# Where the second gather's rows lie within blocks of 32 partitions

## The chip, the cores and the metric

The kernel runs on one core of a Trainium2 chip. The metric is the time of one execution on the device, in microseconds (us). Before the change three runs took 2975.83 to 2976.99 us, with a median of 2976.5 us.

## What is computed

Two layers on 256 tokens of width 2048, everything in float32. The first is a convolution block with a feed-forward block; the second is attention, a pooling branch and, at its end, a layer of small experts. Only this last layer is touched by the change. For each token and each of 8 heads it chooses 16 of 16384 experts, takes a row of 2048 numbers for each from a table U, and, with the weights so found, adds up the same rows of a second table V:

```python
u = jnp.take(expert_u, idx, axis=0)
a = jnp.einsum('thkd,td->thk', u, xb)
hid = jax.nn.gelu(a) * g
vsel = jnp.take(expert_v, idx, axis=0)
return jnp.einsum('thk,thkd->td', hid, vsel)
```

That is 256 x 8 x 16 = 32768 (token, head, slot) choices, each with a row of U and the same row of V, 8 KB each.

## The kernel before, in words

**Which rows are gathered.** The kernel handles the 16384 experts in two ways. Those of the last 40 of 128 key groups (index 88 x 128 = 11264 and up) are computed densely: their rows of U and V are streamed as whole panels of 1 MB by SyncE's queue (line 526) and multiplied by TensorE (lines 2363 and 2373). All other choices are gathered row by row. A gather is one indirect transfer of up to 128 rows into a tile of 128 partitions; an index at or over 11264 is out of its bounds, and its row isn't fetched.

**Gathers of U.** GpSimd issues 256 gathers of U (line 638). Number k belongs to group g = k // 4 and fetches one slot of one head for 128 tokens, token p into partition p. VectorE multiplies the tile with the tokens' inputs and sums (`dot`, line 1824), one tile at a time.

**Gathers of V.** GpSimd issues as many gathers of V (line 658), four for a group, each for 32 tokens and the group's four slots: slot s of the four lies in partitions 32 s to 32 s + 31. TensorE multiplies such a tile by a matrix of 128 rows and 32 columns that holds the weights (`spread`), so that each row is added to its token's output (`adds`, line 2418). The two kinds of gathers alternate: U number k, then V number k - 4. In what follows "pair k" is U number k with V number k.

**Batches.** The 16 slots of a head are four batches of four, j = 0 to 3. `four_of(g)` says which head and which batch group g is: the groups go over the heads first, so that groups of one batch follow each other. A group's heads belong to one block of 128 tokens: groups 0 to 31 to the first, 32 to 63 to the second.

**The shift.** Within a block of 32 partitions the V rows don't lie in the order of the tokens: partition p holds the row of token (p + 16) mod 32 of its block. Three places make this so. Line 1795 shuffles the expert indices of a head on VectorE after they are found (`pairs_experts`), line 1873 shuffles the weights of a group in the same way, and lines 1102 and 1109 on ScalarE build the `spread` matrix from a shifted unit matrix. Groups 17 to 31 take another way to the same matrix: line 1157 makes a diagonal of the unshuffled weights, and TensorE turns it over.

**The order of the work.** The routing of a head (its best keys, the pairs, the experts) runs on VectorE. Three heads are routed before the gathers begin; the other 13 are interleaved, one a group with some groups left out (`route_in`), in groups 1 to 6 and on to group 15, the last of their four steps being `pairs_experts`, which ends with line 1795. All engines work in the order in which they are written. A gather of U waits for its index (`expert_ready`) and for a free tile: there are 5 tiles for U, 7 from k = 136 on, and 7 tiles for V, then 8. The dense U panels come in groups 0 to 17, the dense V panels from group 34 on.

Of the kernel before, what the change touches and what calls it, by code (L numbers as in the profile page):

```python
# [33 lines left out]
PH, TOPK, NKEYS = 8, 16, 128  # L34
# [112 lines left out]
    return PH + g % PH, g // PH  # L147


SHIFTED = [(p + 16) % 32 for p in range(32)]  # L150


def route_in(g):
# [90 lines left out]
def two_layers(nc, stream, dense_u, columns, x, meta, b_out, g_mix_post, g_ffn, g_ffn_post, g_norm1, g_norm2, w_forget,  # L244
# [5 lines left out]
    K, Q = 1024, 32  # L250
# [3 lines left out]
    def place(name, shape, offset, dt=f32):  # L254
        assert name not in names
        names.add(name)
        return nc.alloc_sbuf_tensor_at(name, shape, dt, offset=offset)
# [10 lines left out]
    ident = keep("s_ident", [128, 128])  # L268
# [108 lines left out]
    def spot(n):  # L377
        size = (4 * n + 63) // 64 * 64
        for piece in room:
            if piece[0] + size <= piece[1]:  # L380
                piece[0] += size
                return piece[0] - size
        raise MemoryError(n)

    def small(name, n, dt=f32):
        return place(name, [128, n], spot(n), dt)
# [8 lines left out]
    cand = place("s_cand", [128, TOPK * TOPK], pick_at)  # L395
    cand_rest = place("s_cand_rest", [128, TOPK * TOPK], pick_at + 4 * TOPK * TOPK)
    diagonal = [place(f"s_diagonal{i}", [128, 4, Q], pick_at + 512 + 512 * i) for i in range(2)]
    iota_i = small("s_iota_i", NKEYS, mybir.dt.int32)
    iota_f = small("s_iota_f", NKEYS)
    sc_rest = small("s_sc_rest", NKEYS)  # L400
    val = small("s_val", 2 * TOPK)
# [5 lines left out]
    gsum = small("s_gsum", 4)  # L407
    expert_f = [small(f"s_expert_f{i}", TOPK) for i in range(2)]
    expert_v_f = [small(f"s_expert_v_f{i}", TOPK) for i in range(2)]
    shifted = small("s_shifted", Q)  # L410
    u_index = [small(f"s_u_index{i}", TOPK, u32) for i in range(ROUTES)]
    v_index = [small(f"s_v_index{i}", 4 * GROUPS, u32) for i in range(ROUTES)]
    gate_kept = [small(f"s_gate_kept{i}", TOPK) for i in range(ROUTES)]
# [6 lines left out]
    with ExitStack() as ctx:  # L420
# [253 lines left out]
        def _(act):  # L674
# [422 lines left out]

            for q in range(4):
                own = slice(q * Q, (q + 1) * Q)
                for half in range(2):  # L1100
                    from_half = slice(q * Q + (1 - half) * Q // 2, q * Q + (2 - half) * Q // 2)
                    ins = act.activation(shifted[own, half * Q // 2:(half + 1) * Q // 2], ident[own, from_half], ACT.Copy)
            ins.then_inc(shifted_ready, 1)
            act.wait_ge(shifted_ready, 1)

            def one_spread(g, q, s):

                own = slice(q * Q, (q + 1) * Q)
                return act.activation(spread[g % NW][s * Q:(s + 1) * Q, q, :], shifted[own, :], ACT.Copy,  # L1109
                                      scale=hid[g % NH][own, s:s + 1])  # L1110

            def spreads(g):
# [40 lines left out]
            def diagonal_of(g):  # L1153

                act.wait_ge(hid_ready, g + 1)
                for s in range(4):
                    ins = act.activation(diagonal[g % 2][:, s, :], shifted[:, :], ACT.Copy, scale=hid[g % NH][:, s:s + 1])
                ins.then_inc(diagonal_ready, 1)

            def blocks_copied(g):  # L1160
# [60 lines left out]
        def _(dve):  # L1221
# [558 lines left out]
            def pairs_experts(th):  # L1780

                step(dve.tensor_scalar(pos_of[:, 0:TOPK], pos[:, :], 4, None, ALU.logical_shift_right))
                link(dve.tensor_scalar(pos_of[:, TOPK:], pos[:, :], TOPK - 1, None, ALU.bitwise_and))
                both = pick[:, :].rearrange("p (s a) -> p s a", a=TOPK)
                halves = pick[:, :].rearrange("p (h k a) -> p h k a", h=2, a=TOPK)
                link(dve.tensor_tensor(both, iota_f[:, 0:TOPK].unsqueeze(1).to_broadcast([128, 2 * TOPK, TOPK]),
                                       pos_of[:, :].unsqueeze(2).to_broadcast([128, 2 * TOPK, TOPK]), ALU.is_equal))
                link(dve.tensor_tensor(halves, halves, ind[:, :].rearrange("p (h a) -> p h a", h=2).unsqueeze(2).to_broadcast([128, 2, TOPK, TOPK]),
                                       ALU.mult))
                keys_of = picked[th // PH][:, 0:2 * SLOTS].rearrange("p (h s) -> p h s", h=2)[:, :, th % PH * TOPK:(th % PH + 1) * TOPK]  # L1790
                link(dve.tensor_reduce(keys_of, halves, AX.X, ALU.add))
                wait(dve, v_index_ready, th - 1)
                link(dve.scalar_tensor_tensor(expert_f[th % 2][:, :], keys_of[:, 0, :], float(NKEYS), keys_of[:, 1, :], ALU.mult, ALU.add))
                link(dve.tensor_copy(u_index[th][:, :], expert_f[th % 2][:, :]))
                dve.stream_shuffle(expert_v_f[th % 2][:, :], expert_f[th % 2][:, :], SHIFTED).then_inc(expert_ready, 1)

            def gates_softmax(th):
                mine = picked[th // PH][:, 2 * SLOTS + th % PH * TOPK:][:, 0:TOPK]
# [64 lines left out]
            def hidden(g, first=0, end=BATCH):  # L1863

                th, j = four_of(g)
                dve.wait_ge(gelu_ready, g + 2 if first else g + 1)
                mine = hid[g % NH][:, first:end]
                if g in TURNED:
                    dve.tensor_tensor(mine, gelu[g % NH][:, first:end], gate_kept[th][:, j * BATCH + first:j * BATCH + end], ALU.mult)\
                        .then_inc(hid_ready, 1)  # L1870
                else:
                    link(dve.tensor_tensor(mine, gelu[g % NH][:, first:end], gate_kept[th][:, j * BATCH + first:j * BATCH + end], ALU.mult))
                    dve.stream_shuffle(mine, mine, SHIFTED).then_inc(hid_ready, 1)  # L1873


            dve.wait_ge(iota_ready, 1)
# [650 lines left out]
```

## Time and profile before

| what | us |
|---|---|
| median of 3 runs | 2976.5 |
| lowest and highest run | 2975.83, 2976.99 |
| the profiled execution's own time | 2973.8 |
| its span, first to last instruction | 2971.7 |
| first gather issued (of U) | 1804.1 |
| last gather issued (of V) | 2947.6 |
| last row packet of a gather ends, about | 2964 |

The profile is of one execution. Times inside it are counted from its first instruction. PE is TensorE, DVE VectorE, ACT ScalarE, POOL GpSimd, SP SyncE. The transfer engines (DMA) are 16; a "share" of them is the time that their packets took, divided by 16 times the stretch, and can come out slightly above 1. A row of a table is one packet of 8 KB; a row that is out of bounds, and each engine's notice that it is done, is a packet of a few bytes.

### The profile page before, as it was taken

Reading aid. Unit: us, or ns where it says so; the run is one execution under the profiler, and the core shown is the slowest. Engines: PE = TensorE matmul, PEld = TensorE weight load, DVE = VectorE, ACT = ScalarE, POOL = GpSimd, SP = SyncE. Lnnn points to the kernel's source line nnn. Section 1 sums busy time; section 2 is a strip of 40 time slices with the busy share of each in tenths; the row PEclk is TensorE's granted clock in tenths of the full one; section 3 lists DMA queues with packets and bytes.
Section 4 is the critical chain, followed back from the end, with each engine's and each line's share of the span. In section 5 each row is a group of like instructions: output and inputs, shape, how many; then the busy total and the mean of one; then the engine's idle time right before and its main releaser. Section 6 shows DMA issues by size and latency. Waiting matters only on the chain.

```text
span 2971.7 us, 45765 instructions
## 1 busy us (share of the span) xinstructions
PE 2759.5 (93%) x17115; PEld 2063.2 (69%) x17115; DVE 1917.5 (65%) x3302; ACT 1177.4 (40%) x2302; POOL 660.7 (22%) x568
## 2 busy tenths in 40 slices
PE   8999999999999997999999999999998787888885
PEld 7886778888888887989999889677764432222221
DVE  6888566655665556455444557988858885555556
ACT  1003443333333434434333445565556542223333
POOL 0000000000000000040000002454446665555554
PEclk9999999999999998999999999999996679989897
DMA  6432545555555553443455656999999999999998
GB/s 246 142 142 101 209 158 187 193 186 183 189 192 183 186 193 121 165 147 141 173 185 184 249 201 226 365 409 416 413 378 419 401 409 423 423 422 420 419 420 356
DMA packets 131299, 785.53 MB, mean 264 GB/s; under 512 B 34630, under 2 KB 34630, under 8 KB 35846
## 3 DMA queue, kind: packets, MB, share of 16 engines
q1 hardware_dynamic: 55040, 393.16, 36.0%
q0 software_dynamic: 75712, 389.74, 32.4%
q8 instruction: 94, 1.54, 0.2%
q14 instruction: 69, 0.57, 0.1%
q10 hardware_dynamic: 384, 0.52, 0.0%
HBM read 940.23 MB, written 4.19 MB: 318 GB/s over the span
## 4 chain that ended last, share of the span: by engine, by line
PE 62%; DMA 16%; DVE 12%; issue 6%; ACT 2%; POOL 2%; DVEq 1%; POOLq 0%; ACTq 0%
PE bank L1970 10%; PE bank L1964 10%; PE bank L1965 10%; PE bank L1966 10%; DMA s_u<-in_expert_u,s_u_index 10%; DMA s_v<-in_expert_v,s_v_index 6%; PE bank L2363 6%; PE bank L1971 5%; PE bank L2060 4%; DVE s_u L1824 3%; PE bank L2418 3%; PE bank L2373 2%; DVE s_cacc L1333 2%; POOL s_u L638 1%; DVE s_w_lo L1244 1%
## 5 line engine op out<-in xcount | busy, mean ns | idle before, releaser
L1244 DVE TENSOR_TENSOR s_w_lo<-s_raw,s_w_hi 128x2048 fp32r<-128x2048 f32 x258 | 592.6, 2297 | 577.0 <-ACT s_w_hi L685 576.5
L685 ACT ACTIVATE s_w_hi<-s_raw 128x2048 fp32r<-128x2048 f32 x256 | 490.4, 1916 | 750.6 <-PE bank L1966 475.2
L1970 PE MATMUL bank<-s_a,s_w_hi 128*128 128x512 f32 x1408 | 494.3, 394 | 3.2 <-DVE s_w_lo L1244 3.2
L1824 DVE CUSTOM_DVE_ANT_0 s_u<-s_u,s_xn_late 128x1024 f32<-128x1024 f32 x256 | 303.6, 1223 | 221.2 <-DMA s_u<-in_expert_u,s_u_index 195.3
L2418 PE MATMUL bank<-s_v,s_spread 128*32 128x512 f32 x2048 | 312.5, 727 | 142.2 <-DMA s_v<-in_expert_v,s_v_index 106.0
L1971 PE MATMUL bank<-s_a,s_w_lo 128*128 128x256 f32 x1408 | 395.1, 281 | 0.0
L638 POOL DMA_INDIRECT s_u<-in_expert_u,s_u_index x256 | 298.9, 1168 | 381.4 <-DVE s_halfdot L1824 222.4
L658 POOL DMA_INDIRECT s_v<-in_expert_v,s_v_index x256 | 311.5, 1217 | 206.6 <-PE bank L2418 120.3
L1824 DVE CUSTOM_DVE_ANT_0 s_u<-s_u,s_xn 128x1024 f32<-128x1024 f32 x256 | 303.0, 1223 | 46.6 <-DMA s_u<-in_expert_u,s_u_index 40.9
L1964 PE MATMUL bank<-s_a,s_w_hi 128*128 128x256 f32 x1152 | 325.1, 282 | 3.4 <-DVE s_a L1268 1.8
L1965 PE MATMUL bank<-s_a,s_w_hi 128*128 128x256 f32 x1152 | 324.4, 282 | 0.0
L1966 PE MATMUL bank<-s_a,s_w_lo 128*128 128x256 f32 x1152 | 324.0, 281 | 0.0
L1109 ACT ACTIVATE s_spread<-s_shifted,s_hid 32x32 f32<-32x32 f32 x784 | 249.4, 318 | 188.0 <-DVE s_hid L1873 169.0
L1970 PEld LDWEIGHTS bank<-s_a,s_w_hi 128*128 128x128 f32 x1408 | 264.7, 188 | 66.2 <-DVE s_w_lo L1244 6.4
L2418 PEld LDWEIGHTS bank<-s_v,s_spread 128*32 128x32 f32 x2048 | 64.0, 123 | 341.0 <-issue 284.6
L2373 PE MATMUL bank<-s_raw,s_ha 128*32 128x512 f32 x2560 | 297.1, 617 | 0.0
L2363 PE MATMUL bank<-s_xnt,s_raw 128*128 128x256 f32 x1184 | 265.2, 382 | 1.3 <-issue 0.9
L1971 PEld LDWEIGHTS bank<-s_a,s_w_lo 128*128 128x128 f32 x1408 | 264.9, 188 | 0.4
L2363 PEld LDWEIGHTS bank<-s_xnt,s_raw 128*128 128x128 f32 x1184 | 221.9, 190 | 59.6 <-issue 30.9
L2060 PE MATMUL bank<-s_a_f,s_raw 128*128 128x272 f32 x1024 | 235.2, 393 | 2.0 <-DVE s_a_f L1301 1.2
L2373 PEld LDWEIGHTS bank<-s_raw,s_ha 128*32 128x32 f32 x2560 | 94.8, 115 | 202.8 <-issue 202.0
L2060 PEld LDWEIGHTS bank<-s_a_f,s_raw 128*128 128x128 f32 x1024 | 194.4, 190 | 42.6 <-issue 2.6
(332 smaller groups left out, 3912.3 us busy)
## 6 DMA issues: line engine op xcount, KB each, us to landing
s_raw<-in_stream SPq DMA_DIRECT2D x292, 1024.0 KB, 4.8
s_raw<-in_expert_v SPq DMA_DIRECT2D x40, 1024.0 KB
s_raw<-in_dense_u SPq DMA_DIRECT2D x37, 1024.0 KB
s_u<-in_expert_u,s_u_index POOLq DMA_INDIRECT x256
s_v<-in_expert_v,s_v_index POOLq DMA_INDIRECT x256
s_panel_early<-in_dense_u POOLq DMA_DIRECT2D x3, 1024.0 KB, 11.4
s_xres<-in_x SPq DMA_DIRECT2D x2, 1024.0 KB, 5.9
out<-s_out_row SPq DMA_DIRECT2D x24, 64.0 KB
```

The costliest lines, as they stand in the source:

```text
L685: act.activation(w_hi[s % 2][:, :], raw[s][:, :], ACT.Copy).then_inc(hi_ready, 1)
L1244: dve.tensor_tensor(w_lo[s % 2][:, :], raw[s][:, :], w_hi[s % 2][:, :].bitcast(f32), ALU.subtract)\
L1824: ins = dve.tensor_tensor_reduce(out=u_slot[r][:, half], in0=u_slot[r][:, half], in1=xn_late[:, half] if t else xn[:, 0, half], scale=SHRI ...
L1964: pe.matmul(dst, left[0], right[0], start=start, stop=False)
L1965: pe.matmul(dst, left[0], right[1], start=False, stop=False)
L1966: return pe.matmul(dst, left[1], right[0], start=False, stop=stop)
L1970: pe.matmul(dst, left[0], both, start=start, stop=False)
L1971: return pe.matmul(dst[:, 0:T], left[1], both[:, 0], start=False, stop=stop)
L2060: ins = pe.matmul(bank[c][:, 0:L], raw[c % 4][:, k * 128:(k + 1) * 128], a_f[:, k, :], start=k == 0, stop=k == KT - 1)
L2363: ins = pe.matmul(bank[b][:, 0:T], source[:, k * 128:(k + 1) * 128], xnt[:, k, 0:T], start=k == 0, stop=k == KT - 1)
L2373: ins = pe.matmul(bank[4 * t + q][c * Q:(c + 1) * Q, :], ha[:, d, t * 128 + q * Q:t * 128 + (q + 1) * Q], raw[r][:, c * 512:(c + 1) * 512] ...
L2418: ins = pe.matmul(bank[4 * t + q][c * Q:(c + 1) * Q, :], spread[g % NW][:, q, :], v_slot[r][:, c * 512:(c + 1) * 512], start=False, stop=last)
```

## The change

The shift becomes a number for each batch: 16, 8, 24 and 16 for j = 0 to 3. The one shuffle of a head's 16 indices becomes four shuffles of four indices (L1795). The weights of a group are shuffled by its batch's shift (L1873). The shifted unit matrix gives way to two unit matrices side by side, `same_q`, 64 columns wide, out of which a window of 32 columns is read at the batch's shift; it lies where `iota_i` lay, which is no longer used by then. Batches 0 and 3 keep the shift that they had.

```diff
--- before.py
+++ after.py
@@ -147,7 +147,12 @@
     return PH + g % PH, g // PH
 
 
-SHIFTED = [(p + 16) % 32 for p in range(32)]
+SHIFTS = (16, 8, 24, 16)
+
+
+def shifted_by(shift):
+
+    return [(p + shift) % 32 for p in range(32)]
 
 
 def route_in(g):
@@ -395,7 +400,9 @@
     cand = place("s_cand", [128, TOPK * TOPK], pick_at)
     cand_rest = place("s_cand_rest", [128, TOPK * TOPK], pick_at + 4 * TOPK * TOPK)
     diagonal = [place(f"s_diagonal{i}", [128, 4, Q], pick_at + 512 + 512 * i) for i in range(2)]
-    iota_i = small("s_iota_i", NKEYS, mybir.dt.int32)
+    iota_at = spot(NKEYS)
+    iota_i = place("s_iota_i", [128, NKEYS], iota_at, mybir.dt.int32)
+    same_q = place("s_same_q", [128, 2 * Q], iota_at)
     iota_f = small("s_iota_f", NKEYS)
     sc_rest = small("s_sc_rest", NKEYS)
     val = small("s_val", 2 * TOPK)
@@ -407,7 +414,6 @@
     gsum = small("s_gsum", 4)
     expert_f = [small(f"s_expert_f{i}", TOPK) for i in range(2)]
     expert_v_f = [small(f"s_expert_v_f{i}", TOPK) for i in range(2)]
-    shifted = small("s_shifted", Q)
     u_index = [small(f"s_u_index{i}", TOPK, u32) for i in range(ROUTES)]
     v_index = [small(f"s_v_index{i}", 4 * GROUPS, u32) for i in range(ROUTES)]
     gate_kept = [small(f"s_gate_kept{i}", TOPK) for i in range(ROUTES)]
@@ -1097,16 +1103,15 @@
 
             for q in range(4):
                 own = slice(q * Q, (q + 1) * Q)
-                for half in range(2):
-                    from_half = slice(q * Q + (1 - half) * Q // 2, q * Q + (2 - half) * Q // 2)
-                    ins = act.activation(shifted[own, half * Q // 2:(half + 1) * Q // 2], ident[own, from_half], ACT.Copy)
+                for twice in range(2):
+                    ins = act.activation(same_q[own, twice * Q:(twice + 1) * Q], ident[own, own], ACT.Copy)
             ins.then_inc(shifted_ready, 1)
             act.wait_ge(shifted_ready, 1)
 
             def one_spread(g, q, s):
 
                 own = slice(q * Q, (q + 1) * Q)
-                return act.activation(spread[g % NW][s * Q:(s + 1) * Q, q, :], shifted[own, :], ACT.Copy,
+                return act.activation(spread[g % NW][s * Q:(s + 1) * Q, q, :], same_q[own, Q - SHIFTS[four_of(g)[1]]:2 * Q - SHIFTS[four_of(g)[1]]], ACT.Copy,
                                       scale=hid[g % NH][own, s:s + 1])
 
             def spreads(g):
@@ -1154,7 +1159,7 @@
 
                 act.wait_ge(hid_ready, g + 1)
                 for s in range(4):
-                    ins = act.activation(diagonal[g % 2][:, s, :], shifted[:, :], ACT.Copy, scale=hid[g % NH][:, s:s + 1])
+                    ins = act.activation(diagonal[g % 2][:, s, :], same_q[:, SHIFTS[four_of(g)[1]]:Q + SHIFTS[four_of(g)[1]]], ACT.Copy, scale=hid[g % NH][:, s:s + 1])
                 ins.then_inc(diagonal_ready, 1)
 
             def blocks_copied(g):
@@ -1792,7 +1797,10 @@
                 wait(dve, v_index_ready, th - 1)
                 link(dve.scalar_tensor_tensor(expert_f[th % 2][:, :], keys_of[:, 0, :], float(NKEYS), keys_of[:, 1, :], ALU.mult, ALU.add))
                 link(dve.tensor_copy(u_index[th][:, :], expert_f[th % 2][:, :]))
-                dve.stream_shuffle(expert_v_f[th % 2][:, :], expert_f[th % 2][:, :], SHIFTED).then_inc(expert_ready, 1)
+                for j in range(GROUPS):
+                    four = slice(j * BATCH, (j + 1) * BATCH)
+                    ins = dve.stream_shuffle(expert_v_f[th % 2][:, four], expert_f[th % 2][:, four], shifted_by(SHIFTS[j]))
+                ins.then_inc(expert_ready, 1)
 
             def gates_softmax(th):
                 mine = picked[th // PH][:, 2 * SLOTS + th % PH * TOPK:][:, 0:TOPK]
@@ -1870,7 +1878,7 @@
                         .then_inc(hid_ready, 1)
                 else:
                     link(dve.tensor_tensor(mine, gelu[g % NH][:, first:end], gate_kept[th][:, j * BATCH + first:j * BATCH + end], ALU.mult))
-                    dve.stream_shuffle(mine, mine, SHIFTED).then_inc(hid_ready, 1)
+                    dve.stream_shuffle(mine, mine, shifted_by(SHIFTS[j])).then_inc(hid_ready, 1)
 
 
             dve.wait_ge(iota_ready, 1)
```

## Rows read from the trace of the kernel before

**Rows 1.** The page, transfer engines' busy tenths and rate in 40 slices of the span
```profile
DMA  6432545555555553443455656999999999999998
GB/s 246 142 142 101 209 158 187 193 186 183 189 192 183 186 193 121 165 147 141 173 185 184 249 201 226 365 409 416 413 378 419 401 409 423 423 422 420 419 420 356
```

**Rows 2.** Busy time by stage (first line names the columns)
```profile
core 0: us, PE busy (x) PEld busy (x) DVE busy (x) ACT busy (x) POOL busy (x), PEclk, DMA share, GB/s
1850.00:2222.00 372.00, 362.23 (x1899) 262.41 (x1895) 308.38 (x886) 207.85 (x665) 172.34 (x148) 0.98 0.99 395
2222.00:2964.00 742.00, 598.32 (x4554) 217.87 (x4550) 480.67 (x968) 285.99 (x898) 426.58 (x356) 0.83 1.00 413
1851.00:1990.00 139.00, 133.75 (x697) 95.43 (x690) 127.13 (x376) 73.72 (x240) 62.50 (x56) 0.99 0.97 376
1990.00:2200.00 210.00, 208.71 (x1102) 153.20 (x1106) 166.21 (x479) 115.00 (x368) 98.54 (x85) 1.00 1.01 415
```

**Rows 3.** Chain that ended last, shares by line: 1851 to 1990, then 1990 to 2200
```profile
by line: DVE s_u L1824 43.2%; issue 12.1%; DVE s_ind L1762 3.2%; DVE s_ind L1757 3.0%; DVE s_pick L1786 3.0%; DVE s_pick L1788 3.0%; DVE s_picked L1791 3.0%; DVE s_val L1760 2.6%; DVE s_sc_rest L1758 2.4%; DVE s_val L1755 2.3%; DVE s_pos L1
...
by line: PE bank L2363 77.9%; PE bank L2418 17.0%; DMA s_raw<-in_dense_u 4.6%; issue 0.3%; PE bank L2384 0.3%
```

**Rows 4.** Waits from 1850 to 1990: who for whom, us in total, times, longest
```profile
POOL s_u L638 <- DVE s_halfdot L1824: 62.9, 24, 3.9
PEld bank L2418 <- ACT s_spread L1109: 11.0, 9, 2.4
```

**Rows 5.** Chain that ended last, shares by line: 2200 to 2450, then 2450 to 2930
```profile
by line: DMA s_u<-in_expert_u,s_u_index 35.0%; issue 14.8%; DMA s_v<-in_expert_v,s_v_index 12.7%; POOL s_u L638 9.1%; DVE s_u L1824 7.9%; PE bank L2398 6.8%; PE bank L2418 6.2%; POOL s_v L658 3.3%; PE bank L2363 2.8%; ACT s_one_key_more L11
...
by line: DMA s_u<-in_expert_u,s_u_index 36.3%; DMA s_v<-in_expert_v,s_v_index 33.1%; PE bank L2373 12.5%; issue 5.6%; PE bank L2418 4.8%; DVE s_u L1824 3.5%; POOL s_u L638 3.1%; POOL s_v L658 1.7%; POOLq L638 0.1%; POOLq L658 0.1%; POOLq L6
```

**Rows 6.** Transfer queues, 2500 to 2900: packets, then queue, packets, MB, share of 16 engines
```profile
DMA packets 30940, 168.40 MB, mean 421 GB/s; under 512 B 10412, under 2 KB 10412, under 8 KB 10412
q0 software_dynamic: 26056, 132.54, 80.0%
q1 hardware_dynamic: 4849, 35.38, 21.0%
```

**Rows 7.** Packets from 2222 to 2964, then from 1850 to 2222
```profile
DMA packets 58180, 306.43 MB, mean 413 GB/s; under 512 B 20437, under 2 KB 20437, under 8 KB 20949
...
DMA packets 26469, 146.81 MB, mean 395 GB/s; under 512 B 8567, under 2 KB 8567, under 8 KB 8567
```

**Rows 8.** Transfer queues around the first gather of U, 1807 to 1811
```profile
DMA packets 170, 0.99 MB, mean 248 GB/s; under 512 B 49, under 2 KB 49, under 8 KB 49
q0 software_dynamic: 144, 0.78, 60.7%
```

**Rows 9.** VectorE in order of time: start us, us, engine, line, operation
```profile
1838.12 0.28 DVE L1757 FIND_INDEX8 s_ind<-s_val,s_score 128x8 uint32<-128x128 f32 x1
1838.32 0.07 DVE L1758 MATCH_VALUE_LOAD s_sc_rest<-s_val,s_score 128x8 f32 x1
...
1845.87 0.01 DVE L1795 LOAD_MASK_SELECT s_expert_v_f<-s_expert_f  x1
1845.87 0.17 DVE L1795 STREAM_SHUFFLE s_expert_v_f<-s_expert_f 128x16 f32<-128x16 f32 x1
1845.95 4.48 DVE L1900 TENSOR_TENSOR s_xnt<-s_a 128x2048 f32<-128x2048 f32 x2
```

**Rows 10.** Lines 1795 and 1873: duration ns min/median/max, first and last start us, forms
```profile
L1795 DVE STREAM_SHUFFLE s_expert_v_f<-s_expert_f x16: 168/170/171, 1803.0 to 2158.0; 128x16 f32<-128x16 f32 x16
...
L1873 DVE LOAD_MASK_SELECT s_hid<-s_hid x50: 14/14/14, 1863.0 to 2961.3; - x50
L1873 DVE STREAM_SHUFFLE s_hid<-s_hid x50: 151/154/157, 1863.0 to 2961.3; 128x4 f32<-128x4 f32 x48, 128x3 f32<-128x3 f32 x1, 128x1 f32<-128x1 f32 x1
```

**Rows 11.** ScalarE's lines 1102 and 1109, the same columns
```profile
L1102 ACT ACTIVATE s_shifted<-s_ident x8: 194/205/216, 1851.6 to 1852.7; 32x16 f32<-32x16 f32 x8
...
L1109 ACT ACTIVATE s_spread<-s_shifted,s_hid x784: 315/318/324, 1863.2 to 2962.5; 32x32 f32<-32x32 f32 x196
```

## The prediction, made before the changed kernel ran

> **What bounds the kernel now.** I first read the slices of the page for where the change can act at all. The gathers begin in slice 25 of 40, and from slice 26 on the transfer engines are at nine tenths busy, with about 420 GB/s in the last third [rows 1]. I then split the time after the first dots into two stages by the windows view [rows 2]. From 1850 to 2222 everything is nearly full: TensorE is busy for 362 of 372 us, the transfer engines have a share of 0.99, VectorE 308 us. From 2222 to 2964 only the transfer engines are full: share 1.00, TensorE 598 of 742 us, VectorE 481.
>
> Next comes the chain of waits, stage by stage. From 1851 to 1990 it is VectorE's: dots and the routing of heads, with no transfer among its larger parts. From 1990 to 2200 it is TensorE's, 95% by its lines 2363 and 2418 [rows 3]. That VectorE leads first is seen also in the waits: GpSimd stands 62.9 us for dots before it may issue a gather of U, and TensorE waits for spread matrices, 11.0 us in one row [rows 4]. After 2200 transfers lead, 48% of the chain to 2450 and 69% from 2450 to 2930; in the earlier part GpSimd, VectorE, TensorE and the pauses between instructions hold the rest [rows 5].
>
> What does a full transfer engine mean here? From 2500 to 2900 queue 1 moved 35.38 MB, or 4319 packets of 8 KB, in 21.0% of 16 x 400 us; that is 0.31 us for a packet, and sixteen engines at that pace give the 421 GB/s that the window shows [rows 6]. A row therefore costs its engine 0.31 us, and a row out of bounds next to nothing. At 421 GB/s, the 306.43 MB of the second stage would take 728 us and took 742, so 14 us of all engines' time are lost; in the first stage 146.81 MB would take 349 of 372 us [rows 7].
>
> **Which engine fetches which row.** No view tells an engine, but the packets themselves do where a gather stands alone. The first gather of U is 144 packets, 128 rows and 16 notices [rows 8]. Ordered so that each packet starts where another ended, they fall into strings of eight long or short packets and a notice. Of the thirteen strings that came out whole, eleven have the pattern that the routing gives if engine i (0 to 7) takes partitions 4i to 4i + 3 and 32 more, and engine 8 + i the same 64 further on; eight neighbouring partitions to an engine explain five of them, every sixteenth partition four. I take the first.
>
> So the shift decides which engine fetches a token's V row, and the loads can be counted. I worked out the reference's own choice of experts on its inputs: 22933 of the 32768 rows of each table are in bounds, 11.2 rows an engine for each pair of gathers, but not evenly. Over the pairs from 80 on (issued from 2222 on), the mean engine has 1966.5 rows and the fullest 2003 before. The excess of 36.5 rows is 11.3 us at 0.31, most of the 14 us lost: in this stage the fullest engine sets the end.
>
> **The change, part by part.** Three shuffles more for each of 16 heads, on VectorE. Before, the shuffle starts at 1845.87 and the next instruction at 1845.95, 0.08 us on, though it lasts 0.17 [rows 9]; the form with four columns lasts 0.154, after a mask load of 0.014 [rows 10]. A state load behind a search of 0.28 us also starts 0.08 before its end [rows 9], so I take 0.08 + 0.014 = 0.094 us for a further shuffle; the bounds are 0.08 and the full 0.168. Who waits: the index of U and the notice `expert_ready` now come after all four, and the dots behind them. The first two heads are routed while TensorE is busy with the query weights; the gathers that they start wait for later things. The third head and those of groups 1 to 6, seven heads, stand on VectorE's chain up to 1990. The others fall under TensorE's chain to 2200, which covers 0.3 us a head; without that cover nine heads would cost 2.5 us. Sum: 7 x 3 x 0.094 = **2.0 us**, bounds 1.7 and 3.5. Can it be nothing? Only if TensorE, busy for 133.75 of these 139 us, hid it all [rows 2]; I let the range reach there.
>
> ScalarE. Eight copies of 32x16 at 205 ns become eight of 32x32; the row of line 1109 bounds one at 318, so 0.9 us more. They start at 1851.6, and the first spread at 1863.2 [rows 11]: zero; without that gap, the 0.9. Spreads and diagonals keep count and size and only read from another column: zero. The weights' shuffle keeps its count with another mask, GpSimd issues the same gathers in the same order, and SyncE's queue isn't passed by anything: zero. The tile that takes iota_i's place is written long after its reader: zero.
>
> The engines' loads. Only batches 1 and 2 move, so half the V gathers: pairs 12 to 35 and 68 to 107 in the first token block, 160 to 223 in the second. U and the totals of all engines stay; what changes is the fullest engine. From pair 80 on it goes from 2003 to 2014 rows, plus 11, or +3.4 us. From pair 144 on, where transfers hold most of the chain, it goes from 1293 to 1299, plus 6, or +1.9 us. I take the middle, 8.5 rows: **2.6 us**, since before 2450 half of the chain isn't a transfer [rows 5]. Bounds: over all 256 pairs the fullest goes from 2943 to 2938, or -1.6 us; and if tiles are too few for an engine to run ahead, each stretch has its own fullest engine: over stretches of 12 pairs the excesses sum to 170.5 rows before and 185.7 after, plus 15.2, or +4.7 us. In the first stage (pairs 0 to 79) the fullest goes from 940 to 934, -1.9 us if transfers led there; by the chain they don't, so I take zero.
>
> Sum: 2.0 + 2.6 = **4.6 us** more. The profiled execution, 2973.8 with a span of 2971.7, would become 2978.4; it lies 2.7 below the median of the runs, 2976.5, and the forecast in those terms is 2981.0 us. That is +0.15%. About 0.2%, or 6 us, is what a measurement of this kernel can tell from no change, so I call the forecast "no change".
>
> **The rivals.** First, few tiles (slower). Five U tiles up to pair 136 and seven after it let no engine run far ahead. If a local fullest engine holds up the gathers of each dozen pairs, the load term is 4.7, and with the shuffles the time is 2976.5 + 6.7 = 2983.2 us. For it: the rate isn't always full in the second stage, the slice from 2303 to 2377 has 401 GB/s, not 420 [rows 1]. Against: the sum of local excesses, 170 rows or 53 us, is far above the 14 us lost [rows 7]; engines do run ahead. It decides from a load term of 4 us on. The same sign comes with shuffles at their full price.
>
> Second, one ceiling for all. If not the engines but a limit common to them holds the rate at 421 GB/s, the fullest engine's rows don't matter and only the shuffles count: 2976.5 + 2.0 = 2978.5 us. For it: the rate stands at 420 to 424 over most of the second stage whatever is transferred. Against: lost time and fullest engine's excess agree (14 and 11 us). The Trainium skill, page "DMA: Bandwidth & Descriptors", section "Where 436 GB/s comes from", has such common limits, about 358 GB/s for a core's share of HBM and 435 for the fabric. By the first no balance could matter; the trace runs at 421, above it, so it doesn't hold here, and the second isn't reached.
>
> Third, another assignment of rows to engines (faster). If every sixteenth partition shared an engine, a shift of 16 would put U and V rows of the same tokens on the same engine; the fullest would have 2144 rows from pair 80 on before and 2100 after, -13.6 us, and the time would be 2976.5 + 2.0 - 13.6 = 2964.9 us. It decides from some 26 rows fewer on. Against: four strings of thirteen.
>
> Fourth, the change doesn't do what it says, the row order staying as it was: only the 2.0 us, 2978.5. The shift stands in all three places in the diff, with one sign, so this is small.
>
> **How the numbers follow.** Forecast 0.47, common ceiling 0.10, shift without effect 0.03: together 0.60 for "within 0.2%". Few tiles 0.32: slower. Another assignment 0.08: faster. The forecast's own range is 2976.5 - 1.9 to 2976.5 + 3.5 + 4.7, or 2974.6 to 2984.7. The range given reaches 2 us beyond on both sides, 2973 to 2987, to take in the few-tiles case with dear shuffles and a first stage that gains; it leaves out the third rival and little else.
>
> **What would show it.** Line 1795 should have 64 shuffles of 128x4, starting 0.08 to 0.17 us apart, and the first dots about 0.3 us later. At 1990 TensorE's chain should begin some 2 us later than before. The second stage should last 742 us plus 2 to 4, with the same megabytes and a mean rate 0.3 to 0.5% lower; the rate between 2500 and 2900 should stay near 421. Wrong would be: a second stage that is shorter (third rival, or a load count that misses what delays a gather), or more than 5 us longer (few tiles), or a first stage that changes by more than 4 us either way, which would mean that the chain of that stage isn't what I read.

## The result, and the profile after

The changed kernel is slower: 2986.2 us, median of 8 runs (2981.9 to 2986.8), against 2976.2 us for 8 runs of the kernel before beside them. The ratio is 1.0034, with a 95% interval of 1.0025 to 1.0042, so 7 to 13 us more, about 10. The profiled execution took 2986.44 us with a span of 2984.4, 12.7 above the span before.

Where the time went is seen in the same order as before. The page's two lines on transfers, of the changed kernel, answer to [rows 1]:

```profile
DMA  6433545555555553444555656999999999999998
GB/s 245 141 141 110 205 157 191 183 189 191 184 190 189 184 194 120 166 144 142 179 185 185 239 198 244 378 411 414 409 369 422 396 406 423 422 414 413 412 417 326
```

Most slices of the second stage are as they were, but the four from 2611 us on have 414, 413, 412 and 417 where before they had 422, 420, 419 and 420. The stages, in the columns of [rows 2]:

```profile
1850.00:2222.00 372.00, 359.98 (x1887) 262.48 (x1882) 308.07 (x962) 207.26 (x661) 170.05 (x147) 0.98 0.98 393
2222.00:2964.00 742.00, 599.21 (x4526) 222.81 (x4518) 476.13 (x952) 280.88 (x882) 424.03 (x357) 0.82 1.01 412
1851.00:1990.00 139.00, 132.50 (x688) 95.17 (x688) 127.67 (x412) 72.99 (x236) 62.59 (x55) 0.99 0.97 377
1990.00:2200.00 210.00, 207.72 (x1094) 153.00 (x1094) 167.79 (x522) 114.40 (x366) 97.67 (x84) 1.00 1.01 413
```

The first stage hardly differs: 393 against 395 GB/s, TensorE and VectorE busy as before. In the second, the rate is 412 for 413 within the same 742 us, and the stage isn't over then: the last row of a gather has landed at 2977.0, where before it had at 2965.9. The chain of waits of the changed kernel, from 2200 to 2450 and from 2450 to 2930, in place of [rows 5]:

```profile
by line: DMA s_v<-in_expert_v,s_v_index 29.8%; DMA s_u<-in_expert_u,s_u_index 23.2%; PE bank L2406 12.8%; PE bank L2426 8.7%; DVE s_u L1832 7.2%; issue 5.2%; POOL s_u L644 3.0%; PE bank L2371 2.8%; PE bank L2381 2.8%; ACT s_one_key_more L11
...
by line: DMA s_u<-in_expert_u,s_u_index 53.6%; DMA s_v<-in_expert_v,s_v_index 24.4%; PE bank L2381 7.0%; issue 4.8%; DVE s_u L1832 4.0%; PE bank L2426 3.3%; POOL s_u L644 3.1%; POOL s_v L664 1.5%; POOLq L644 0.1%; POOLq L664 0.1%; DVE s_hal
```

The transfers' part of the chain from 2450 on rose from 69% to 78%, and it is gathers of U that took more, 54% for 36%. In the stretch where the rate had been 421 [rows 6] it is 416:

```profile
DMA packets 30616, 166.56 MB, mean 416 GB/s; under 512 B 10312, under 2 KB 10312, under 8 KB 10312
q0 software_dynamic: 25829, 131.48, 80.0%
q1 hardware_dynamic: 4752, 34.61, 20.6%
```

The streamed panels' packets cost what they did: on queue 1, 34.61 MB are 4225 packets in 20.6% of 6400 us, again 0.31 us each. The gathers' packets can be read one by one in the trace: from 2540 to 2810 a row's packet takes 309 ns at the median and at the 95th percentile in both kernels. A working engine isn't slower, then, and the lost time would be that of engines with no work at hand; the last section has a sign of it. A view of both kernels in three parts of the second stage puts a place to it. The columns are those of [rows 2]; first the kernel before:

```profile
core 0: us, PE busy (x) PEld busy (x) DVE busy (x) ACT busy (x) POOL busy (x), PEclk, DMA share, GB/s
2220.00:2540.00 320.00, 257.05 (x1707) 116.89 (x1702) 238.95 (x473) 154.37 (x475) 202.66 (x170) 0.75 1.01 410
2540.00:2810.00 270.00, 229.50 (x1976) 70.22 (x1968) 148.70 (x300) 79.44 (x255) 142.19 (x121) 0.93 1.01 421
2810.00:2964.00 154.00, 113.78 (x884) 31.15 (x888) 95.02 (x197) 53.14 (x171) 82.80 (x66) 0.81 0.98 403
```

then the changed one:

```profile
2220.00:2540.00 320.00, 257.69 (x1667) 121.81 (x1670) 237.93 (x474) 152.32 (x469) 203.78 (x168) 0.75 1.00 408
2540.00:2810.00 270.00, 228.25 (x1952) 68.53 (x1948) 147.06 (x299) 80.71 (x260) 136.09 (x121) 0.91 1.01 415
2810.00:2964.00 154.00, 115.27 (x924) 33.01 (x916) 93.10 (x187) 49.82 (x160) 84.16 (x70) 0.84 1.01 416
```

From 2540 to 2810 the rate fell from 421 to 415 GB/s, which is 1.4%, or 3.9 us of work not done in 270. These are the times of pairs 160 to 219, as nearly as can be (the dots of line 1824, four instructions to a pair, number 637 up to 2540 and 240 more up to 2810), and pairs 160 to 223 are the ones that the change moves in the second token block:

```profile
core 0: us, DVE busy (x), PEclk, DMA share, GB/s
1850.00:2220.00 370.00, 180.60 (x305) 0.99 0.99 395
2220.00:2540.00 320.00, 196.99 (x332) 0.75 1.01 410
2540.00:2810.00 270.00, 142.87 (x240) 0.93 1.01 421
```

After 2810 the changed kernel is still at 416 where the one before was running out (403). The small steps that were added on VectorE, last, in order of time (start, us, engine, line, operation), in place of [rows 9]:

```profile
1845.23 0.15 DVE L1802 STREAM_SHUFFLE s_expert_v_f<-s_expert_f 128x4 f32<-128x4 f32 x1
1845.31 0.15 DVE L1802 STREAM_SHUFFLE s_expert_v_f<-s_expert_f 128x4 f32<-128x4 f32 x1
1845.39 0.15 DVE L1802 STREAM_SHUFFLE s_expert_v_f<-s_expert_f 128x4 f32<-128x4 f32 x1
1845.47 0.15 DVE L1802 STREAM_SHUFFLE s_expert_v_f<-s_expert_f 128x4 f32<-128x4 f32 x1
1845.54 4.48 DVE L1908 TENSOR_TENSOR s_xnt<-s_a 128x2048 f32<-128x2048 f32 x2
```

Four shuffles, 0.08 us apart; from the first to the next instruction it is 0.31 us, where it was 0.08.

### The profile page after: what moved, and what is told of

Its sections match the earlier page's. It is cut to its first block, busy times and chain, and to the rows that moved or that the text cites. A ratio compares the mean times of both kernels' runs of the same rounds, so it can differ in the third digit from the quotient of the medians.

```text
span 2984.4 us, 45861 instructions
## 1 busy us (share of the span) xinstructions
PE 2766.8 (93%) x17115; PEld 2069.6 (69%) x17115; DVE 1920.1 (64%) x3398; ACT 1177.9 (39%) x2302; POOL 656.3 (22%) x568
## 4 chain that ended last, share of the span: by engine, by line
PE 60%; DMA 19%; DVE 12%; issue 5%; ACT 2%; POOL 1%; DVEq 1%; POOLq 0%; SPq 0%; ACTq 0%
DMA s_u<-in_expert_u,s_u_index 11%; PE bank L1978 10%; PE bank L1972 10%; PE bank L1973 10%; PE bank L1974 10%; DMA s_v<-in_expert_v,s_v_index 6%; PE bank L2371 5%; PE bank L1979 5%; PE bank L2068 4%; DVE s_u L1832 3%; PE bank L2426 3%; DVE s_cacc L1338 2%; PE bank L2381 1%; DVE s_w_lo L1249 1%; DVE s_yrow L1511 1%
## 5 line engine op out<-in xcount | busy, mean ns | idle before, releaser
L644 POOL DMA_INDIRECT s_u<-in_expert_u,s_u_index x256 | 288.4, 1127 | 382.1 <-DVE s_halfdot L1832 220.5
L664 POOL DMA_INDIRECT s_v<-in_expert_v,s_v_index x256 | 317.6, 1241 | 223.2 <-PE bank L2426 136.7
L1114 ACT ACTIVATE s_spread<-s_same_q,s_hid 32x32 f32<-32x32 f32 x784 | 249.4, 318 | 179.5 <-DVE s_hid L1881 168.1
## 6 DMA issues: line engine op xcount, KB each, us to landing
s_u<-in_expert_u,s_u_index POOLq DMA_INDIRECT x256, 21.8
```

## The experiments

All are the changed kernel with other shifts, or with another number of shuffles. "Before" is the kernel before, run beside each on the same chip (medians 2974.8 to 2975.5 us); 0.001 in a ratio is 3.0 us. A figure in us behind a ratio is worked out from it in this way.

### Is it the rows, or the code around them?

```diff
-SHIFTS = (16, 8, 24, 16)
+SHIFTS = (16, 16, 16, 16)
```

> The changed code with the shift of 16 in all four batches: the four shuffles and the double unit matrix stay, the rows lie as before the change. Theory (the loss of 10 us is the fullest transfer engines' rows): the time is that of before, within 3 us, since the 0.3 us that the shuffles add per head are made up where VectorE isn't the one waited for. Rival (the added shuffles or the moved tiles cost it): the time stays within 3 us of the changed kernel, some 10 us above before.

Measured: 2978.6 us, ratio 1.0009 (1.0000 to 1.0018), 2.7 us above before. With the rows back in their old places some 7 of the 10 us are gone. A shift moves rows only within a gather, so each gather fetches the same rows in both versions; what differs is the partition, and with it the engine. The rate from 2540 to 2810 is back at 421:

```profile
2220.00:2540.00 320.00, 262.84 (x1687) 124.57 (x1690) 240.05 (x478) 154.96 (x477) 199.29 (x169) 0.74 1.00 409
2540.00:2810.00 270.00, 230.69 (x2000) 70.99 (x1992) 148.74 (x301) 81.21 (x261) 140.78 (x122) 0.92 1.01 421
2810.00:2964.00 154.00, 112.44 (x880) 29.92 (x880) 96.42 (x200) 51.99 (x168) 81.70 (x67) 0.81 0.99 407
```

The 2.7 us that stay were divided by two more. The first gives this version a single shuffle again:

```diff
-for j in range(GROUPS):
-    four = slice(j * BATCH, (j + 1) * BATCH)
-    ins = dve.stream_shuffle(expert_v_f[th % 2][:, four], expert_f[th % 2][:, four], shifted_by(SHIFTS[j]))
-ins.then_inc(expert_ready, 1)
+dve.stream_shuffle(expert_v_f[th % 2][:, :], expert_f[th % 2][:, :], shifted_by(16)).then_inc(expert_ready, 1)
```

> 16 throughout with one shuffle of a head's indices, as before the change, but with the double unit matrix and its window. Theory (the 2.7 us of the four-shuffle version are three shuffles at some 0.085 us in seven heads, 1.8 us, and noise): within 2 us of before, and 1 to 3 us under the four-shuffle version. Rival (the window into the double matrix, or where it lies, costs): 2 to 3 us above before.

Measured: 2975.9 us, ratio 1.0001 (0.9992 to 1.0010). The double unit matrix costs nothing that can be told from before. The second has sixteen shuffles of a column each:

```diff
-for j in range(GROUPS):
-    four = slice(j * BATCH, (j + 1) * BATCH)
-    ins = dve.stream_shuffle(expert_v_f[th % 2][:, four], expert_f[th % 2][:, four], shifted_by(SHIFTS[j]))
+for slot in range(TOPK):
+    one = slice(slot, slot + 1)
+    ins = dve.stream_shuffle(expert_v_f[th % 2][:, one], expert_f[th % 2][:, one], shifted_by(16))
```

> 16 throughout, but the shuffle of a head's indices cut in sixteen of one column each, in place of four: twelve more for a head. The four-shuffle version measured 2.7 us above before, with an interval that reaches 0. If a further shuffle costs 0.08 us on VectorE's chain in seven heads, this one is 7 x 12 x 0.08 = 6.7 us above the four-shuffle version, 9 to 10 above before. If TensorE, nearly full in the same stage, hides them, it is within 3 us of the four-shuffle version.

Measured: 2984.7 us, ratio 1.0032 (1.0019 to 1.0044), 9.5 above before and 6.8 above four shuffles. That is 0.081 us for each of 7 x 12 shuffles, near the 0.075 from one to the next in its own order of time (first and last of the sixteen shuffles of the third head, and the next instruction):

```profile
1846.54 0.15 DVE L1802 STREAM_SHUFFLE s_expert_v_f<-s_expert_f 128x1 f32<-128x1 f32 x1
...
1847.67 0.15 DVE L1802 STREAM_SHUFFLE s_expert_v_f<-s_expert_f 128x1 f32<-128x1 f32 x1
1847.74 2.28 DVE L1908 TENSOR_TENSOR s_xnt<-s_a 128x2048 f32<-128x2048 f32 x1
```

So the shuffles of the change cost about 2 us by this price (7 x 3 x 0.081 = 1.7) and 2.7 as measured by the version with four (0 to 5.4 by its interval), and the rows the rest, about 7.4. Where 2.7 us are taken off in what follows, they are no surer than that.

### Which rows

The first token block alone has the new shifts, then the second alone (here and below, ScalarE's two windows are read by the same table):

```diff
-SHIFTS = (16, 8, 24, 16)
+SHIFTS = ((16, 8, 24, 16), (16, 16, 16, 16))
...
-shifted_by(SHIFTS[j])
+shifted_by(SHIFTS[th // PH][j])
```

> New shifts for the heads of the first 128 tokens, 16 throughout for the second 128. Theory: the dots of the second token block (from about 2400 us on) showed 7 to 8 of the 12 us lost, between pairs 160 and 223, so this one is 2 to 5 us above before. Rival (the loss is spread evenly, or comes from the first stage): 5 us or more of the 10 stay.

Measured: 2978.9 us, ratio 1.0011 (1.0002 to 1.0020), 3.3 above before; less the 2.7 of the shuffles, 0.6.

```diff
+SHIFTS = ((16, 16, 16, 16), (16, 8, 24, 16))
```

> The reverse: 16 for the first 128 tokens, the new shifts for the second 128. Theory: over pairs 144 to 223 the fullest engine has 943 rows in place of 918, 25 rows or 7.7 us at 0.31, and the delay of the dots should appear there alone: 6 to 9 us above before, none of it before pair 160. Rival (whole-stage count of the prediction, plus 11 rows from pair 80 on): at most 3 us above before.

Measured: 2986.9 us, ratio 1.0035 (1.0021 to 1.0049), 10.4 above before; less the shuffles, 7.7. The second block's rows hold the loss, and the count over the whole stage, which the prediction used, doesn't give it. Within the second block, batch 1 alone and batch 2 alone:

```diff
+SHIFTS = ((16, 16, 16, 16), (16, 8, 16, 16))
```

> Of the change only the shift of 8 in batch 1 of the second 128 tokens is kept (pairs 160 to 191); all else 16, four shuffles. By the count engine 12 gets 385 rows there in place of 359, and pairs 160 to 223 have a fullest engine of 752 rows in place of 730, 22 rows or 6.8 us. Theory (fullest engine of that stretch): 6 to 10 us above before, nearly all of the second block's loss. Rival (both batches share the loss): about 6.

```diff
+SHIFTS = ((16, 16, 16, 16), (16, 16, 24, 16))
```

> The other half: only the shift of 24 in batch 2 of the second 128 tokens (pairs 192 to 223); all else 16, four shuffles. By the count pairs 160 to 223 have a fullest engine of 745 rows, 15 more than before (4.6 us), but the fullest over the stage goes down, from 2003 to 2000. Theory (stretch): 5 to 8 us above before. Theory (whole stage): 2 to 3 us, the shuffles alone.

Measured: 2985.7 us for batch 1, ratio 1.0031 (1.0022 to 1.0041), 9.2 above before, 6.5 without the shuffles; 2980.9 us for batch 2, ratio 1.0018 (1.0009 to 1.0027), 5.4 and 2.7. Batch 1 holds most of it: by the count, the shift of 8 gives engine 12 in pairs 160 to 191 385 rows in place of 359. The rates of the three parts agree, first with batch 1 alone, then with batch 2 alone:

```profile
2220.00:2540.00 320.00, 260.44 (x1682) 125.56 (x1685) 240.51 (x478) 154.98 (x476) 198.46 (x168) 0.75 1.00 408
2540.00:2810.00 270.00, 223.88 (x1924) 67.23 (x1920) 146.21 (x294) 77.60 (x250) 135.88 (x119) 0.91 1.01 415
2810.00:2964.00 154.00, 116.10 (x948) 34.29 (x940) 92.59 (x190) 52.75 (x169) 85.72 (x71) 0.86 1.01 418
```

```profile
2220.00:2540.00 320.00, 260.92 (x1692) 118.89 (x1695) 238.97 (x476) 154.24 (x475) 196.71 (x169) 0.73 1.00 409
2540.00:2810.00 270.00, 230.76 (x1996) 71.11 (x1988) 148.44 (x300) 81.86 (x263) 143.72 (x121) 0.91 1.01 420
2810.00:2964.00 154.00, 110.41 (x870) 29.48 (x864) 92.69 (x187) 47.65 (x153) 81.72 (x68) 0.81 1.00 409
```

415 and 420 between 2540 and 2810. Batch 2's 2.7 us lie nearer to the stretch's count (15 rows, 4.6 us) than to the whole stage's, which went down; with an interval as wide as the difference, that alone would not decide.

### The whole stage, or each stretch?

If loads decide, a table of shifts that evens them should gain. Each of the 64 groups got its own:

```diff
-SHIFTS = (16, 8, 24, 16)
+SHIFTS = ((8, 28, 28, 4), (12, 20, 24, 24), (16, 28, 12, 20), (24, 24, 28, 28),
+          (4, 28, 24, 20), (24, 12, 28, 12), (12, 4, 28, 12), (20, 4, 20, 16),
+          (12, 12, 20, 20), (12, 16, 8, 20), (28, 28, 24, 12), (24, 28, 12, 24),
+          (8, 8, 24, 8), (20, 20, 4, 24), (4, 8, 8, 28), (8, 20, 4, 24))
...
-shifted_by(SHIFTS[j])
+shifted_by(SHIFTS[th][j])
```

> Each of the 64 groups has a shift of its own, a multiple of 4, chosen by counting rows on these inputs so that no engine is much fuller than the mean over 8 to 64 pairs in a row (sum of the excesses over stretches of 64 pairs from pair 80 on: 11 us, against 22 before and 29 after the change). Theory (engine loads): 6 to 14 us faster than before. Rival (what costs is that shifts other than 16, or unlike shifts, are in flight together): slower than the changed kernel, or as slow, since nearly all groups now differ from 16 and from their neighbours.

Measured: 2966.5 us, ratio 0.9967 (0.9955 to 0.9979), 9.8 under before in spite of the four shuffles. That rules out the rival: unlike shifts in flight side by side do not make it slower, and the gain was forecast from the count of who gets the rows. Two tables then set the two counts against each other, in the same form as the one above:

```diff
-SHIFTS = (16, 8, 24, 16)
+SHIFTS = ((16, 16, 16, 16), (16, 16, 16, 16), (16, 16, 16, 16), (16, 16, 16, 12),
+          (16, 16, 0, 28), (16, 16, 4, 8), (16, 8, 24, 8), (16, 8, 0, 4),
+          (16, 20, 20, 0), (0, 16, 24, 12), (24, 0, 4, 4), (0, 16, 16, 8),
+          (24, 28, 28, 16), (16, 4, 12, 20), (28, 24, 16, 0), (12, 28, 8, 16))
```

> A shift for each group, chosen by counting so that from pair 80 on the fullest engine has as many rows in all as before the change (2003), but every stretch has a much fuller engine of its own: the excesses over stretches of 64 pairs sum to 46 us (before 22, changed kernel 29), over 32 pairs to 61 us (34, 39). Theory A (each stretch's own fullest engine sets its pace, since tiles are few): some 20 to 30 us slower than before. Theory B (the fullest engine over the whole stage sets the end): as the version with 16 throughout and four shuffles, about 3 us above before.

```diff
-SHIFTS = (16, 8, 24, 16)
+SHIFTS = ((24, 4, 8, 20), (8, 16, 4, 12), (12, 12, 28, 8), (28, 24, 28, 8),
+          (4, 8, 16, 12), (20, 20, 4, 20), (16, 16, 28, 24), (28, 0, 28, 12),
+          (24, 12, 24, 12), (4, 4, 4, 28), (20, 20, 28, 4), (28, 24, 24, 8),
+          (24, 4, 16, 16), (4, 12, 4, 4), (20, 16, 20, 20), (20, 24, 24, 8))
```

> The reverse: the excesses over stretches of 12, 16, 32 and 64 pairs are those of before (56, 50, 34 and 22 us), but they fall on the same engine, which from pair 80 on has 2054 rows in place of 2003, 51 more or 16 us. Theory A (stretches): about 3 us above before, as with 16 throughout. Theory B (whole stage): 15 to 20 us above before.

Measured: 2983.3 us with the stretches made worse and the whole kept, ratio 1.0026 (1.0016 to 1.0036), 7.7 above before, 5.0 without the shuffles. And 2987.3 us with the whole made worse and the stretches kept, ratio 1.0040 (1.0026 to 1.0053), 11.9 and 9.2. Neither theory has its figure: A foresaw 20 to 30 and 3, B 3 and 15 to 20. Both counts matter, each less than alone. When they come due is seen in the three parts of the second stage, first with worse stretches:

```profile
2220.00:2540.00 320.00, 255.60 (x1643) 121.13 (x1642) 233.84 (x464) 151.70 (x466) 197.65 (x165) 0.74 1.00 406
2540.00:2810.00 270.00, 231.45 (x1976) 70.17 (x1980) 152.14 (x310) 79.63 (x256) 141.91 (x122) 0.91 1.01 417
2810.00:2964.00 154.00, 115.61 (x932) 32.35 (x924) 94.12 (x189) 52.73 (x169) 80.99 (x71) 0.86 1.01 412
```

The rate is below that of 16 throughout in the first part (406 for 409) and in the second (417 for 421), and not at the end (412 for 407). With one engine fuller over the whole stage:

```profile
2220.00:2540.00 320.00, 258.84 (x1726) 118.00 (x1722) 238.05 (x476) 155.48 (x479) 207.96 (x170) 0.76 1.00 409
2540.00:2810.00 270.00, 227.17 (x1956) 67.75 (x1948) 148.38 (x300) 79.42 (x255) 145.37 (x122) 0.92 1.01 422
2810.00:2964.00 154.00, 111.34 (x856) 29.53 (x857) 91.01 (x183) 47.64 (x153) 78.29 (x67) 0.81 0.99 401
```

Here the rate is full until 2810 (409 and 422, as with 16 throughout), and low at the end, 401, with 20 us still to go. As I read it, the fullest engine runs further and further behind while tiles let the others run on, and its backlog is waited for at the close; which engine was behind was not seen.

### A version that beats both

One shift for a head keeps a single shuffle:

```diff
-SHIFTS = (16, 8, 24, 16)
+SHIFTS = (8, 12, 20, 24, 12, 12, 4, 20, 20, 20, 12, 24, 8, 12, 28, 12)
...
-for j in range(GROUPS):
-    four = slice(j * BATCH, (j + 1) * BATCH)
-    ins = dve.stream_shuffle(expert_v_f[th % 2][:, four], expert_f[th % 2][:, four], shifted_by(SHIFTS[j]))
-ins.then_inc(expert_ready, 1)
+dve.stream_shuffle(expert_v_f[th % 2][:, :], expert_f[th % 2][:, :], shifted_by(SHIFTS[th])).then_inc(expert_ready, 1)
...
-shifted_by(SHIFTS[j])
+shifted_by(SHIFTS[th])
```

> One shift for each of the 16 heads, in all its batches, and so one shuffle of a head's indices again in place of four; chosen by counting rows on these inputs (excess over stretches of 64 pairs 15.8 us, before 21.8; fullest engine from pair 80 on 5.4 us over the mean, before 11.3). Theory: 6 to 8 us faster than before by the loads, with no cost of shuffles; 2 to 5 us less gain than the version with a shift for each group, plus 2 to 3 us for the three shuffles saved, so about level with it. Rival (the per-group version gained by something else than loads): within 3 us of before.

Measured: 2966.8 us, ratio 0.9974 (0.9963 to 0.9985), 7.7 under before.

```diff
+SHIFTS = (8, 12, 12, 24, 12, 12, 4, 20, 20, 20, 12, 8, 8, 12, 28, 12)
```

> As the version with one shift for each head and one shuffle, with two heads' shifts chosen anew: the count was made along the longest run of rows, one engine after another, where going over to another engine skips six pairs of gathers. By that count 9.6 us under before, the first per-head version 8.1. Theory: 8 to 11 us faster than before, level with or 1 to 2 us under the first per-head version and the per-group version. Rival (such fine counts say nothing): anywhere from 5 to 10 us faster.

Measured: 2965.1 us, ratio 0.9965 (0.9953 to 0.9977), 10.4 under before and some 21 under the changed kernel. Its second stage:

```profile
2220.00:2540.00 320.00, 259.24 (x1794) 120.44 (x1790) 242.74 (x481) 155.13 (x479) 207.20 (x174) 0.79 1.01 417
2540.00:2810.00 270.00, 225.50 (x1924) 67.92 (x1920) 150.81 (x308) 79.97 (x257) 140.10 (x121) 0.91 1.02 423
2810.00:2964.00 154.00, 110.44 (x876) 30.03 (x868) 92.13 (x188) 52.40 (x169) 76.71 (x62) 0.83 0.95 394
```

417 GB/s in the first part, where the kernel before had 410, and 394 at the end because the work runs out sooner. It must be said that this table, as the others, was chosen on the routing of these inputs; other inputs would fill other engines.

### All loads side by side

Counts are from pair 80 on, in us at 0.309 a row: the rows that the fullest engine has over the mean engine, averaged over all stretches of 64 pairs and scaled to the 176 pairs, and the same over the whole stage. The last column is the ratio in us, less 2.7 where the version has four shuffles.

| rows as in | stretches of 64 | whole stage | us against before |
|---|---|---|---|
| before | 21.8 | 11.3 | 0 |
| changed kernel | 29.0 | 14.7 | +7.4 |
| first block new | 21.2 | 10.0 | +0.6 |
| second block new | 29.4 | 16.2 | +7.7 |
| its batch 1 alone | 28.7 | 12.5 | +6.5 |
| its batch 2 alone | 24.0 | 10.4 | +2.7 |
| shift for each group | 11.2 | 5.4 | -12.5 |
| shift for each head, first | 15.8 | 5.4 | -7.7 |
| shift for each head, second | 14.1 | 5.4 | -10.4 |
| stretches worse | 46.2 | 11.3 | +5.0 |
| whole worse | 21.9 | 27.0 | +9.2 |

For all but the last two, which were made to pull the counts apart, the measured difference is that of the stretches of 64 pairs to within 3 us, which is as near as the runs can tell. The length was taken when the result was known, and it isn't fixed by these runs: stretches of 48 pairs, counted in the same way, fit as well.

## Why the prediction was right or wrong

**The range held, the likeliest case did not.** 2986.2 lies inside 2973 to 2987, but only by the 2 us that were added as a margin: the sum of the upper bounds was 2984.7, and that with shuffles at 3.5 us, which measured 1.7 to 2.7. That it held is luck in part, since the load term, 7.4 us, is outside its own bounds (-1.6 to 4.7). And the forecast was "no change" at 2981.0, while the loss, +0.34%, is more than the 0.2% that the prediction itself took for none. What came is the first rival, few tiles (0.32), whose 2983.2 is the nearest of the named times; it was itself too small by 3 us. Two of the signs that the prediction named agree with that rival: the second stage was 11 us longer, where more than 5 was to mean few tiles, and the rate from 2500 to 2900 did not stay at 421 but fell to 416.

**The shuffles: right.** 2.0 us were predicted, from 0.094 us each; their price measured 0.081, and their sum 1.7 to 2.7. That TensorE might hide them was left open, and the sixteen-shuffle version, 9.5 us above before, shows that it does not. ScalarE and the double matrix were costed at zero, and the version with one shuffle is at 1.0001.

**The engine map: right, as far as loads can tell.** It was read out of one gather's packets. The Trainium skill, page "DMA: Bandwidth & Descriptors", section "The descriptor swizzle", gives the same map for full transfers to 128 partitions, and these runs agree for gathers with rows left out: the changes in load counted by that map go with the measured times. Tables chosen by it gained 8 to 10 us, and those chosen to lose lost; the third rival's map, by which the change was to gain 13.6 us, is out. So is the runner-up, eight neighbouring partitions to an engine: counted so in stretches of 64 pairs, the change would lose 1.6 us, where it lost 7.4, and the second table of one shift for a head would lose 1.9, where it gained 10.4. Out, too, is the second rival, the common ceiling: the rate from 2540 to 2810 is 423 or 415 GB/s by the choice of shifts alone. That the change does what it says is shown by the same.

**The load term: this is the step that failed.** "I take the middle, 8.5 rows" gave 2.6 us, and the rows cost 7.4. The step counted one fullest engine, from pair 80 or from 144 to the end. That is right only if the fullest engine of a part is also that of the whole. Before, it was engine 8 from pair 144 on; the change made it engine 12 for the pairs 144 to 223 (943 rows, for 918 of engine 8 before), and left engine 8 the fullest of the rest, 375 of pairs 224 to 255, which the change doesn't touch. Counted to the end, the two partly cancel, to plus 6. Counted in their own stretch, the moved pairs are 25 rows or 7.7 us worse, and that is what was measured (7.7 with the second block alone) and where (421 to 415 GB/s from 2540 to 2810). The prediction had the means: its own bound by stretches of 12 pairs was the right kind of count, though with stretches so short that their excesses, 53 us, came out far above the 14 us lost, and for that it was argued away. (Averaged over all places where a stretch of 12 can begin, that count is 182 rows before and 198 after, in place of 170.5 and 185.7; the difference, 5.0 us, is much the same.)

**The first stage: right.** The fullest engine's six rows fewer there were taken for nothing since VectorE and TensorE lead; the first block's rows alone are at +0.6 us without the shuffles.

**What stays open.** Neither count holds by itself: with worse stretches 5.0 us were lost where the stretches of 64 count 24.4, and with a worse whole 9.2 where the whole counts 15.7. How far one engine may fall behind before the dots stop for it was not measured; a version with more tiles was not tried, so that the tiles are what holds the other engines up is argued and not shown.

## What to carry to other kernels

Here the transfer engines were full, each fetched the rows of fixed partitions, and part of each gather's rows was left out; the time then followed the engine with most rows left. In such a kernel count the rows for each engine, stretch by stretch and not only in all: a table that left the whole as it was and made the stretches worse cost 5.0 us. Evening the loads by where rows lie cost no instruction with one shift for each head and gave 8 to 10 us of 2976, though it is tied to the inputs on which it was counted.

## What the runs showed that had not been expected

The mean busy share of the transfer engines does not show this loss: it is 1.01 from 2540 to 2810 before and after, at 421 and 415 GB/s, and from 2500 to 2900 queue 0 has 80.0% in both, with 132.54 MB before [rows 6] and 131.48 after. The rate is the figure to read. The packets themselves tell why: in that stretch nearly all packets of 8 KB take 309 ns, but 156 of 13632 take over 340 ns in the changed kernel, where before it was 52 of 13847. What they take above 309 comes to 4.1 us in the mean of the 16 engines, against 1.5. Such long packets, up to 1360 ns, also begin the first gather of U, which finds the engines without gathers' rows, so they are probably those with which an engine starts again after it had run dry. They go with the loads: the version with one engine fuller over the whole stage has 49 from 2540 to 2810 and 159 from 2810 to 2950, that with 16 throughout 69 and 47, the second table of one shift for a head 22 and 13.

The order in which a backlog comes due had not been expected either: an engine with 51 rows too many over 176 pairs left the rate at 422 until 2810, some 170 us before the end.
